# A Hymba-style layer on one core: the experts' second matrix loaded as 2 MB transfers and worked off in two groups of 8 MB

## The reference

```python
x = x + mixed
x = x + hier_moe(rms_norm(x, norm2_g[l]), w_group[l], w_router[l], w1[l], w3[l], w2[l])

def hier_moe(h, w_group, w_router, w1, w3, w2):
    ...
    comb = jnp.sum(jax.nn.one_hot(expert_id, N_EXPERTS, dtype=jnp.float32) * top_w[..., None], axis=1)
    a = jnp.einsum('nd,edf->nef', hf, w1)
    b = jnp.einsum('nd,edf->nef', hf, w3)
    y = jnp.einsum('nef,efd->nd', jax.nn.silu(a) * b * comb[..., None].astype(h.dtype), w2)
```

## Time and profile before

| | |
|---|---|
| median of 3 runs | 1426.6 us (1425.24 to 1427.34) |
| the profiled execution | 1425.02 us |
| its span in the profile | 1422.8 us |
| PE busy | 1048.7 us (74%) |
| DVE busy | 385.9 us (27%) |
| ACT busy | 277.3 us (19%) |
| bytes moved by DMA | 481.54 MB, mean 338 GB/s |
| mean granted TensorE clock | 0.878 of full speed |

### The profile page before, as it was taken

How to read it: one execution, slowest core, us unless ns; L and a number is a source line. 1 busy time by engine, 2 the same in 40 slices (tenths; PEclk the granted TensorE clock), 3 DMA queues, 4 the chain that set the end, 5 groups by cost and what they waited for, 6 DMA issues and landing times.

```text
span 1422.8 us, 15298 instructions
## 1 busy us (share of the span) xinstructions
PE 1048.7 (74%) x5978; PEld 586.6 (41%) x5978; DVE 385.9 (27%) x549; ACT 277.3 (19%) x433; POOL 62.4 (4%) x46
## 2 busy tenths in 40 slices
PE   7999999999996766567567566656747655675665
PEld 6988878888885413123113111311312311131111
DVE  4548875546654002012011001201201100110111
ACT  5545455446442001001001000100100000010000
POOL 0000261400100000000000000000000000000000
PEclk9999999999997888888797888888878887887878
DMA  8745545544647699999999999999999999999995
GB/s 271 243 148 162 194 148 171 176 154 153 230 162 295 254 421 421 422 421 423 420 423 421 422 421 423 421 422 421 423 422 422 422 422 422 422 422 422 421 421 234
DMA packets 95801, 481.54 MB, mean 338 GB/s; under 512 B 7656, under 2 KB 11904, under 8 KB 46480
## 3 DMA queue, kind: packets, MB, share of 16 engines
q1 hardware_dynamic: 95152, 478.91, 84.2%
q0 software_dynamic: 608, 2.07, 0.4%
HBM read 478.85 MB, written 2.10 MB: 338 GB/s over the span
## 4 chain that ended last, share of the span: by engine, by line
DMA 49%; PE 43%; SPq 3%; DVE 3%; issue 2%; ACT 1%; ACTq 0%; DVEq 0%
DMA ring<-w_dram 48%; PE ps L1377 10%; PE ps L1138 8%; PE ps L1139 8%; PE ps L1140 8%; SPq L327 3%; PE ps L1411 3%; DVE w_lo L704 1%; PE ps L1154 1%; PE ps L1339 1%; DMA xs<-x_dram 1%; PE ps L1427 1%; PE ps L1359 1%; PE ps L1244 0%; PE ps L1170 0%
## 5 line engine op out<-in xcount | busy, mean ns | idle before, releaser
L1377 PE MATMUL ps<-ring,flat 128*32 128x512 f32 x2048 | 329.5, 803 | 237.7 <-DMA ring<-w_dram 236.7
L1377 PEld LDWEIGHTS ps<-ring,flat 128*32 128x32 f32 x2048 | 89.7, 141 | 474.5 <-issue 474.5
L1138 PE MATMUL ps<-w_hi,zT_hi 128*128 128x512 f32 (+2 forms) x576 | 221.5, 385 | 1.7 <-DVE w_lo L704 1.7
L1139 PE MATMUL ps<-w_lo,zT_hi 128*128 128x512 f32 (+2 forms) x576 | 218.6, 379 | 0.0
L1140 PE MATMUL ps<-w_hi,zT_lo 128*128 128x512 f32 (+2 forms) x576 | 218.5, 379 | 0.0
L704 DVE TENSOR_TENSOR w_lo<-ring,w_hi 128x1024 fp32r<-128x1024 f32 (+2 forms) x144 | 180.8, 1275 | 137.0 <-ACT w_hi L445 136.4
L1411 PE MATMUL ps<-ring,flat 128*32 128x512 f32 x1024 | 144.3, 714 | 99.3 <-DMA ring<-w_dram 98.7
L1069 DVE TENSOR_TENSOR xs<-xs,ps 128x512 f32<-128x512 f32 x72 | 49.5, 687 | 561.4 <-PE ps L1359 522.2
L445 ACT CAST w_hi<-ring 128x1024 fp32r<-128x1024 f32 (+2 forms) x144 | 143.4, 1016 | 103.8 <-PE ps L1140 97.3
L650 ACT ACTIVATE flat<-ps 128x512 f32<-128x512 f32 x8 | 4.8, 597 | 612.9 <-PE ps L1377 612.9
L1411 PEld LDWEIGHTS ps<-ring,flat 128*32 128x32 f32 x1024 | 38.9, 128 | 199.5 <-issue 196.8
(11 more groups left out here) (183 smaller groups left out, 464.7 us busy)
## 6 DMA issues: line engine op xcount, KB each, us to landing
ring<-w_dram SPq DMA_DIRECT2D x384, 1024.0 KB, 19.0
ring<-w_in_dram SPq DMA_DIRECT2D x48, 1024.0 KB, 5.0
ring<-w_out_dram SPq DMA_DIRECT2D x16, 1024.0 KB, 5.1
ring<-w_in_dram SPq DMA_DIRECT2D x4, 608.0 KB, 7.8
ring<-w_in_dram SPq DMA_DIRECT2D x4, 576.0 KB, 3.9
xs<-x_dram SPq DMA_DIRECT2D x4, 512.0 KB, 9.2
out_dram<-xs SPq DMA_DIRECT2D x4, 512.0 KB, 2.6
flat<-norm_g_dram POOLq DMA_DIRECT2D x1, 1024.0 KB, 7.2
```

Source lines behind the costliest of these rows:

```text
L1138: mm(b, zh[:, c, t], wh, start=(c == 0), stop=False)
L1139: mm(b, zh[:, c, t], wl, start=False, stop=False)
L1377: last = mm(ps[part, up, :], h_e[:, c, part], w[m][:, cc * NB:(cc + 1) * NB], start=(c == 0), stop=(c == C - 1))
```

## The change

The 16 chunks of w2 are loaded by 8 transfers of 2 MB per team. Each fills two neighbouring slots, with a row of 16 KB per partition: 4096 numbers that lie in one piece in w2, which are the quarters j = 0 and 1 (or 2 and 3) of one expert. Only even chunk numbers of w2 carry a load (`carries`), and the load waits until both slots are free. The slots' semaphores count accordingly. TensorE works w2 off in two halves: it waits for four transfers (8 MB), issues 32 matmuls (x64 in the profile) for two quarters, and adds 8 to `ring_used` with the last one. The products, their number and their order are the same; w1, w3 and all other stages are as before.

```diff
 def chunk_landed(k):
 
-    return 16 * (k // RING + 1)
+    return 16 * sum(carries(n) for n in range(k + 1) if chunk_slot(n) == chunk_slot(k))
+
+
+def carries(k):
+
+    return k < UP_CHUNKS or k % 2 == 0
...
             def load(k, src):
-                sp.dma_start(ring[:, chunk_slot(k), :], src.rearrange("o p n -> (o p) n")).then_inc(landed[chunk_slot(k)], 16)
+                at = ring[:, chunk_slot(k), :]
+                if k >= UP_CHUNKS:
+                    at = ring[:, chunk_slot(k):chunk_slot(k) + 2, :].rearrange("p s n -> p (s n)")
+                sp.dma_start(at, src.rearrange("o p n -> (o p) n")).then_inc(landed[chunk_slot(k)], 16)
...
-                q = (k - UP_CHUNKS) // TEAM
-                return w2_v[bass.ds(number * TEAM + m, 1), :, q * 2048:(q + 1) * 2048]
+                half, m = (k - UP_CHUNKS) // (2 * TEAM), (k - UP_CHUNKS) // 2 % TEAM
+                return w2_v[bass.ds(number * TEAM + m, 1), :, half * 4096:(half + 1) * 4096]
 
             def team(it, number):
 
-                for k in range(TEAM_CHUNKS):
-                    sp.wait_ge(ring_used, it * TEAM_CHUNKS + (k - RING + 1))
+                for k in filter(carries, range(TEAM_CHUNKS)):
+                    sp.wait_ge(ring_used, it * TEAM_CHUNKS + (k - RING + (1 if k < UP_CHUNKS else 2)))
                     load(k, chunk(k, number))
...
                 pe.wait_ge(hm_T_ready, it + 1)
-                for j in range(J):
-                    w = [landed_now(it, UP_CHUNKS + TEAM * j + m) for m in range(TEAM)]
-                    for n in range(4):
-                        for m in range(TEAM):
-                            part = slice(SLOTS * m, SLOTS * (m + 1))
-                            last = mm(ps[part, 4 + n, :], hm_T[:, j, part], w[m][:, n * NB:(n + 1) * NB],
-                                      start=(j == 0), stop=(j == J - 1))
-                    last.then_inc(ring_used, TEAM)
+                for half in range(2):
+                    for m in range(TEAM):
+                        landed_now(it, UP_CHUNKS + 2 * (TEAM * half + m))
+                    for j in (2 * half, 2 * half + 1):
+                        for n in range(4):
+                            for m in range(TEAM):
+                                part = slice(SLOTS * m, SLOTS * (m + 1))
+                                slot = chunk_slot(UP_CHUNKS + 2 * (TEAM * half + m)) + j % 2
+                                last = mm(ps[part, 4 + n, :], hm_T[:, j, part], ring[:, slot, n * NB:(n + 1) * NB],
+                                          start=(j == 0), stop=(j == J - 1))
+                    last.then_inc(ring_used, 2 * TEAM)
```

More of the change, by code:

```diff
@@ L357, in _ @@
                 load(k, chunk(k, 0))
-            for k in range(RING, TEAM_CHUNKS):
-                sp.wait_ge(ring_used, k - RING + 1)
+            for k in filter(carries, range(RING, TEAM_CHUNKS)):
+                sp.wait_ge(ring_used, k - RING + (1 if k < UP_CHUNKS else 2))
                 load(k, chunk(k, 0))
@@ L1363, in landed_now @@
                 k = n
-                pe.wait_ge(landed[chunk_slot(k)], it * (16 * TEAM_CHUNKS // RING) + chunk_landed(k))
+                per_team = sum(16 for i in range(TEAM_CHUNKS) if carries(i) and chunk_slot(i) == chunk_slot(k))
+                pe.wait_ge(landed[chunk_slot(k)], it * per_team + chunk_landed(k))
                 return ring[:, chunk_slot(k), :]
```

## The result

The changed kernel takes 1457.5 us (median of 4 runs, 1456.8 to 1457.7), the kernel before 1425.9 us in the same comparison. The ratio is 1.022, with a 95% interval of 1.0204 to 1.0235: slower by 2.2%, 31.6 us. The forecast was 1461 us, with a range of 1440 to 1475. The profiled execution took 1457.7 us, with a span of 1455.5.

What follows compares the result with a forecast made beforehand. The prediction took the expert stage's stream of loads as the bound. Stops +37.3, tail +3.7 and rows -5 gave +36.0 us on 1425.0, forecast as 1461 us, with a range for 8 in 10 of 1440 to 1475.

Steps and rivals of the forecast that it cites:

- What bounds the kernel: Expert stage: a stream of 384 loads of 1 MB at 422 GB/s; TensorE follows, 9.94 us per 4 MB.
- what stays: w1 and w3 groups, gather, scatter, all matmuls and everything before the experts stay; extra register steps are hidden.
- Step 1, the length of the hold: w2 halves: 64 matmuls hold 8 of the ring's 12 MB for 9.00 us, with 4 MB left in the queue.
- C: Time TensorE takes for one w2 half of 64 matmuls: 5.56 + 3.44 = 9.00 us.
- The rival of a half at half clock: w2 halves: TensorE stays at half clock, about 13.7 us per half; 1537 us in all, chance 0.03.
- the bound of 9.65: Upper bound on a w2 half's time: slowest first group 6.21 + 3.44 = 9.65 us.
- Step 2, the restart: Load queue after each half: restarting it empty costs 3.4 us, each half delays 2.49 us, 15 times: +37.3 us.
- The lower bound, 23.1: Load queue stops, with the restart judged from one load's 4.9 us: 1.54 us per half, 23.1 us in all.
- a cheaper restart: Rival at the load queue's stops: each half's delay is C - 7.46, +21.8 us in total, 1447 us; chance 0.14.
- Step 3, the tail: After the last landing: TensorE's work grows from 5.34 us to 9.00, +3.7 us.
- Step 4, rows of 16 KB: w2 loads: longer rows save between nothing and 17 us; -5 us taken.
- no gain from long rows: Rival at the w2 loads: long rows save nothing, steps 1 to 3 alone give +41.0, 1466 us; chance 0.12.

Runs made afterwards that it cites:

- the seven other runs: The seven follow-up kernels, each a variant of the kernel before or of the changed kernel; they measured from 1424.8 to 1566.0 us.
- doubled halves: Changed kernel with every w2 matmul issued twice, same loads, waits and releases: 1566.0 us, ratio 1.0994 to the changed kernel's.
- halves with 1 MB loads: Changed kernel's two halves of 8 MB, but loaded as before in sixteen transfers of 1 MB with 8 KB rows: 1460.8 us, ratio 1.0244.

## Why the prediction was right, step by step

*What bounds the kernel* and *what stays* held: everything came through the stream's stops, its pace and the tail.

*Step 1, the length of the hold.* C was forecast at 9.00 us. Part 5 of the changed kernel's page gives 145.5 / 16 = 9.09:

```profile
L1423 PE MATMUL ps<-ring,flat 128*32 128x512 f32 x1024 | 145.5, 732 | 145.7 <-DMA ring<-w_dram 145.7
```

The single halves lie between 8.42 and 9.98 us. The long pause of 12 to 13 us ahead of the second halves did not make them slower: they took 8.42 to 8.79 us in the first seven teams, the first halves 8.69 to 9.71 after pauses of some 5 us. The rival of a half at half clock did not occur. Three halves lay above the bound of 9.65 (9.67, 9.71 and 9.98). That bound took 6.21 us for the slowest group; the timeline of before has groups of up to 6.59 us, which would have made it 10.03. It also has 29 single groups of 3.64 us, not 28, which moves C by 0.03. The lower edge of the forecast's own range comes to 1451 by its own terms, not 1452. Nothing else rests on these two.

*Step 2, the restart.* This is the term that was mis-sized. The one restart in the trace of before took 13.37 us from release to the fourth landing, and I took it for all. The 15 restarts of the changed kernel took 12.65 us in the mean (12.3 to 12.95), whether two loads of 2 MB or four of 1 MB came first. That is 0.72 us less, 10.8 us in all. I had argued that it was "this very sequence of four loads into an empty queue", but the first restart was slow in the changed kernel too (472.12 + 3.64 to 489.32: 13.56), and in the seven other runs (13.7 to 14.0). The doubled halves show that it makes no difference whether the queue was dry for 1.5 or for 7.5 us. But ahead of the first restart no bytes had moved for some 13 us (in the trace of before, from 463 to 476), and there the first release gave back 4 MB and not 8. What sets this restart apart was not tested. The stops cost 29.2 us (17.1 + 9.9, and 2.2 that the long rows of the second halves are taken to have hidden), against 37.3 forecast. The difference of 8.1 is these 10.8, less the 2.2, which the forecast counts in step 4, and less 0.5, because the fifteen halves with loads behind them took 9.03 us and not 9.00. The lower bound, 23.1, stood on the other side of it. Measured against the rival *a cheaper restart*, the truth lies between the two and nearer to it: by 19.88 - 12.65 a hold costs from about 7.2 us on, where I had 6.51 and the rival 7.46.
The excess over the transfer is 12.65 - 9.94 = 2.7 us. The Trainium skill ("DMA: Bandwidth & Descriptors", Anatomy of one DMA) has about 2.0 us of fixed cost, a fit for transfers that GpSimd issues, where these are issued by SyncE. The measured 2.7 lies as far above it as below my 3.4.

*Step 3, the tail.* Forecast +3.7, measured +6.2. The last half took 9.98 us, not 9.00, which makes +4.6. And the last scatter took 9.21 us where before had 7.70, which makes +1.5: TensorE began it at half clock. A window at its start in the changed kernel, and then one in the kernel before (length; busy time of PE, PEld, DVE, ACT and POOL; granted clock; DMA share; GB/s):

```profile
1442.50:1447.00 4.50, 4.49 (x7) 1.83 (x8) 1.37 (x2) 0.00 (x0) 0.00 (x0) 0.62 0.00 0
```

```profile
1411.00:1415.00 4.00, 3.64 (x8) 1.27 (x8) 1.95 (x3) 0.30 (x1) 0.00 (x0) 1.00 0.02 9
```

I had not looked at what follows the last group. The pause for ACT's copies is the same (2.17 and 2.16 us), and in before the clock was up when it ended. That these 1.5 us belong to the change is not shown. The run that waits for 4 MB and gives back 8 has the tail of before, 5.34 us of matmuls and 2.16 of pause, and its scatter took 9.37 us, at 0.62 of the clock for its first 4.5 us; the one with the doubled halves has 15.22 us of matmuls in its last half and a scatter of 7.68. So the part of the tail that the change surely brought is 4.6 us, of which I forecast 3.7.

*Step 4, rows of 16 KB.* Forecast -5; 16 x 0.28 = -4.5. Half of this is measured directly, the 2.3 us ahead of the eight first halves. For the second halves, whose stretches hold a stop, I take the same. The halves with 1 MB loads were 3.3 us slower as a whole. The line through rows of 2 and 8 KB, which gave 17, was indeed far too steep. The pace of 428 GB/s stays below the ceiling of 435 in the Trainium skill ("DMA: Bandwidth & Descriptors", Where 436 GB/s comes from). The rival *no gain from long rows* fell: 1.4% of pace came from the row's length alone. The Trainium skill (same page, Rules for kernel authors) asks for 1 MiB or more per transfer, which the loads have both before and after.

*The sum.* 29.2 + 6.2 - 4.5 = 30.9, with 0.5 and 1.3 us of other delays 32.7, against 36.0 forecast. Too high a restart and too low a tail cancelled in part: the 3.3 us between them are 8.1 too many for the stops, less 2.5 for the tail, 0.5 for the rows and 1.8 that I had no term for. The mechanism was right; that the total came so near is in part luck.

## What to carry to other kernels

In a stream bound by loads, count what is left in the queue when a consumer starts on a group, not how long the consumer is idle: here 4 MB (9.9 us) hid holds of 5.1 to 6.6 us but for single delays of 1.1 us at most, while from 8.4 us on every further microsecond was paid in full, 15 times. Between 6.6 and 8.4 no hold was measured; the restart's length puts the edge at about 7.2 us. If a larger wait is wanted for the sake of longer rows, give the buffers back in the old portions: the same wait with the old release cost 5 us in place of 32. And the last group of a program stands on the path with its whole length (5.34, 9.98 and 15.22 us here), so it is the first to make small; no run tried one smaller than 4 MB.

## What the runs showed of the hardware that I had not expected

- A restart of the load queue costs 2.7 us beyond the transfer (12.65 us for 4 MB in place of 9.94), whether the queue was dry for 1.5 us or for 7.5. At the start of the experts, after 13 us without bytes, it was 3.4 to 4.0.
- Rows of 16 KB move at 428 GB/s and rows of 8 KB at 422, with transfers of 2 MB in both cases.
- In the last team, the 8 MB up to the sixth group took 20.8 to 21.4 us in the profiles of the changed kernel and of all seven others (21.15 in the changed one, 20.78 in the one with half the matmuls) and 19.83 in that of before, with the DMA engines busy throughout (422 GB/s in the changed kernel). Before has only this one profile, so whether the difference belongs to the kernels or to the execution is open. In that time bytes of later loads moved as well, so one or more of the 16 engines may have fallen behind; which and why was not tested.
